# A hybrid gMLP, retention and pooling backbone: where ScalarE writes the normalised tiles of the pooling layer

## The reference

```python
def _rms_norm(x, gain):
    xf = x.astype(jnp.float32)
    y = xf * lax.rsqrt(jnp.mean(xf * xf, axis=-1, keepdims=True) + EPS)
    return (y * gain.astype(jnp.float32)).astype(x.dtype)

def _pool_mixer(h, w_pool, pool_scale):          # h: normed and modulated tokens
    ...
    for g, w in enumerate(POOL_WINDOWS):         # windows 2, 4, 8, 16
        lo = jnp.clip(t - w // 2, 0, length)
        hi = jnp.clip(t + w // 2, 0, length)
        mean = (csum[:, hi, g] - csum[:, lo, g]) / (hi - lo)
        outs.append(mean - hg[:, :, g])
    pooled = jnp.stack(outs, axis=2).astype(h.dtype)
    y = jnp.einsum('blgc,gcd->blgd', pooled, w_pool).reshape(bsz, length, D_MODEL)
    return y * pool_scale
```

## Time and profile before

| | us |
|---|---|
| median of 3 runs | 2644.5 |
| lowest, highest | 2641.74, 2645.16 |
| the profiled execution | 2645.16 |
| its span in the trace | 2643.4 |
| TensorE busy | 2561.9 (97%) |
| VectorE busy | 1351.4 (51%) |
| ScalarE busy | 593.9 (22%) |
| GpSimd busy | 544.8 (21%) |

### The profile page before, as it was taken

The page is one execution under the profiler, slowest core; times in us unless marked ns, Lnnn a source line. Parts: engine busy times, 40 slices in busy tenths (PEclk is TensorE's granted clock), DMA queues, the critical chain, the costliest instruction groups (busy, mean ns, idle before and its releaser), DMA issues.

```text
span 2643.4 us, 37530 instructions
## 1 busy us (share of the span) xinstructions
PE 2561.9 (97%) x14604; PEld 2240.7 (85%) x14604; DVE 1351.4 (51%) x2366; ACT 593.9 (22%) x982; POOL 544.8 (21%) x230
## 2 busy tenths in 40 slices
PE   7899999979999999999999999999999999999998
PEld 3878899977888888888888888888888888888887
DVE  6635752264385556554556555564444444444445
ACT  3311122142231111111111112751112111121112
POOL 6124321162121212111112111011121211212110
PEclk9999999989999999999999999899999999999999
DMA  7314523274212211211211211011010100101102
GB/s 236 149 67 142 166 96 112 95 265 168 72 33 80 71 56 56 95 56 56 71 56 56 95 56 32 25 32 33 32 48 32 48 32 32 48 32 48 32 32 80
DMA packets 126263, 199.48 MB, mean 75 GB/s; under 512 B 4420, under 2 KB 102504, under 8 KB 125800
## 3 DMA queue, kind: packets, MB, share of 16 engines
q1 hardware_dynamic: 123216, 188.76, 21.1%
q10 hardware_dynamic: 2968, 9.63, 1.2%
HBM read 167.44 MB, written 26.74 MB: 73 GB/s over the span
## 4 chain that ended last, share of the span: by engine, by line
PE 88%; DVE 5%; issue 2%; DMA 2%; ACT 2%; POOL 1%; ACTq 0%; SPq 0%; DVEq 0%; POOLq 0%
PE bank L314 83%; PE bank L1404 1%; PE bank L1432 1%; PE bank L1557 1%; DMA ada_st_in<-in_ada_w_dram 1%; PE bank L1469 1%; DVE ada_acc_in L1053 0%; PE bank L1735 0%; DVE vtok L1107 0%; DMA SB<-state_spill 0%; DVE xgm L1220 0%; POOL ringL L854 0%; DVE h1L L1227 0%; DVE X L1061 0%; ACT pF L736 0%
## 5 line engine op out<-in xcount | busy, mean ns | idle before, releaser
L854 POOL TENSOR_TENSOR ringL<-stage,ringH 128x2048 fp32r<-128x2048 f32 x82 | 392.8, 4790 | 1823.1 <-ACT ringH L532 1823.1
L1061 DVE SCALAR_TENSOR_TENSOR X<-bank,mod,X 128x512 f32<-128x512 f32 (+1 forms) x792 | 515.1, 660 | 363.4 <-PE bank L314 359.1
L314 PE MATMUL bank<-midH,ringH 128*128 128x512 f32 (+1 forms) x1536 | 546.7, 356 | 3.3 <-DVE X L1061 3.3
L314 PE MATMUL bank<-midL,ringH 128*128 128x512 f32 (+1 forms) x1536 | 544.9, 355 | 0.0
L314 PE MATMUL bank<-midH,ringL 128*128 128x512 f32 (+1 forms) x1536 | 544.7, 355 | 0.0
L314 PE MATMUL bank<-hH,ringH 128*128 128x512 f32 (+1 forms) x1248 | 447.2, 358 | 0.2 <-DVE hL L1227 0.2
L314 PE MATMUL bank<-hH,ringL 128*128 128x512 f32 (+1 forms) x1248 | 442.5, 355 | 0.0
L314 PE MATMUL bank<-hL,ringH 128*128 128x512 f32 (+1 forms) x1248 | 442.4, 355 | 0.0
L1336 DVE TENSOR_TENSOR relu<-relu 128x512 f32<-128x512 f32 (+1 forms) x192 | 146.3, 763 | 568.9 <-ACT relu L774 568.8
L774 ACT ACTIVATE relu<-bank 128x512 f32<-128x512 f32 (+1 forms) x192 | 100.9, 527 | 1375.9 <-PE bank L314 1375.9
L314 PEld LDWEIGHTS bank<-midH,ringH 128*128 128x128 f32 x1536 | 291.5, 190 | 46.1 <-DVE X L1061 6.5
(11 more groups left out here) (191 smaller groups left out, 2888.1 us busy)
## 6 DMA issues: line engine op xcount, KB each, us to landing
stage<-in_mlp_w_dram SPq DMA_DIRECT2D x64, 1024.0 KB, 5.3
ada_st_mlp<-in_ada_w_dram SPq DMA_DIRECT2D x18, 1536.0 KB, 8.3
stage<-in_ev_w_in_dram SPq DMA_DIRECT2D x14, 1024.0 KB, 5.1
ada_st_in<-in_ada_w_dram SPq DMA_DIRECT2D x8, 1536.0 KB, 9.5
ada<-in_ada_w_dram SPq DMA_DIRECT2D x8, 1024.0 KB, 13.3
x_spill<-X SPq DMA_DIRECT2D x1, 5120.0 KB, 18.5
gate_spill<-gate_st ACTq DMA_DIRECT2D x8, 640.0 KB, 3.7
gt<-gate_spill SPq DMA_DIRECT2D x20, 256.0 KB, 3.3
```

Of the source, the lines that this page charges most:

```text
L314: mm = nc.tensor.matmul(out, a, b, start=first and n == 0, stop=last and n == 2)
L854: nc.gpsimd.tensor_tensor(ringL[slot][:, :], stage[:, :], ringH[slot][:, :].bitcast(F32), ALU.subtract).then_inc(w_lo, 1)
L1061: V.scalar_tensor_tensor(out=X[:, d, cols(t)], in0=src[:, 0:TB[t][1]], scalar=gate_ap, in1=X[:, d, cols(t)], op0=ALU.mult, op1=ALU.add).th ...
```

## The change

On ScalarE, `pool_tile_hi` of the tiles 2 to 4 and 6 to 8 is issued later: behind the square and the root of the next tile (`FIRST_TILE[1]` is 2, `NT` is 10). Tiles 0 and 1 keep their place; tile 5 follows tile 4 and tile 9 follows tile 8 directly. On VectorE, the reciprocal of tile 2 comes after update 20 and not 19, and its tL after update 21 and not 20. The reciprocal of tile 3 and its tL stay where they were; TensorE's, GpSimd's and SyncE's lists are the same.

```diff
--- before.py
+++ after.py
@@ -85,8 +85,8 @@
 H1_KB = {0: 0, 1: 16, 2: 32}
 HALO = 2 * PADW + P
 LAST_MM_AT = {9: 0, 14: 1, 18: 2, 19: 3, 22: 4, 23: 5}
-LAST_RS_AT = {11: 0, 16: 1, 19: 2, 21: 3}
-LAST_LO_AT = {12: 0, 17: 1, 20: 2, 22: 3}
+LAST_RS_AT = {11: 0, 16: 1, 20: 2, 21: 3}
+LAST_LO_AT = {12: 0, 17: 1, 21: 2, 22: 3}
 POOL_TILE_AT = {("c", 0): 6, ("e", 0): 7, ("e", 1): 8, ("e", 2): 9}
 NORM_AT = {("e", 4): ("tile", 0), ("c", 6): ("tile", 1), ("e", 5): ("row", 0), ("e", 8): ("tile", 2), ("c", 10): ("tile", 3),
            ("e", 9): ("tile", 4), ("c", 11): ("tile", 5), ("e", 10): ("row", 1)}
@@ -804,15 +804,21 @@
         for j in range(6):
             tile_square(2, j)
             pool_sd(j)
-            pool_tile_hi(j)
+            if j < FIRST_TILE[1]:
+                pool_tile_hi(j)
+            elif j > FIRST_TILE[1]:
+                pool_tile_hi(j - 1)
+        pool_tile_hi(5)
         act.wait_ge(gain_ok, 6)
         for n in range(len(UNITS)):
             pooled_hi(n)
             if n < 4:
                 tile_square(2, 6 + n)
                 pool_sd(6 + n)
-                pool_tile_hi(6 + n)
+                if n > 0:
+                    pool_tile_hi(5 + n)
             if n == 3:
+                pool_tile_hi(NT - 1)
                 split_static(U_MLP[1])
             if n == 5:
                 tile_square(3, 0)
```

## The result

| | us |
|---|---|
| median of 5 runs, before | 2643.99 (2641.74 to 2645.16) |
| median of 5 runs, after | 2655.93 (2654.34 to 2659.68) |
| ratio after to before | 1.0052, 95% interval 1.0041 to 1.0063 |
| profiled execution, after | 2655.41, span 2653.6 |
| recorded mean TensorE clock, profiled before and after | 0.988, 0.986 |

What follows compares the result with a forecast made beforehand. Between the two MLPs a chain of short hand-overs was taken to bound the kernel. Rounds of 5.16 us put the weight copy +7.0 or +9.1 later; +8.0 on 2644.5 gave 2652.5 us, range 2648.2 to 2656.8.

Steps and rivals of the forecast that it cites:

- The round: Tiles in two PSUM pairs: the pairs go in turn, one round taking 5.16 us per tile, before 3.3.
- Tiles 2 to 5: First four moved-stage tiles: tile 5 starts at 1659.26 (+3.35), first pF copy at 1665.52 (+5.3 us).
- The copy: Next MLP's weight copy on ScalarE: starts at 1686.4 or 1688.5 against 1679.40, +7.0 or +9.1 us by the clock.
- Removed waits: tH waits for reciprocals on ScalarE: at most 4.4 of 6.8 us go, already inside the sum.
- the 2.67 us from hi of 8 to hi of 9: End of tiles 6 to 9: tile 9's tH comes 2.67 us after tile 8's, its reciprocal queued behind tile 8's tL.
- From there all moves as one piece: Behind the weight copy: order unchanged, a rigid shift to the end, nothing hidden and no further cost.
- The clock term: TensorE ahead of tiles 5 and 6: low clock behind longer stands, so +8.0 taken between +7.0 and +9.1.
- Rival 1: Low clock through all rounds: +1.0 for tiles 8 and 9, +1.5 for one more stretch; +11.6, 2656.1 us; chance 0.12.
- A granted clock low beyond 1675: Changed profile after 1675 us: a low TensorE clock there was listed as a sign the forecast is wrong.

Runs made afterwards that it cites:

- e6: Changed kernel with tL made from tH alone and a PSUM pair freed by tH, not tL (result wrong, time only): 2650.49 us, ratio 1.0016.
- e7: Changed kernel with a third pair of PSUM banks for tile 4, taken from the last four MLP blocks: 2654.48 us, ratio 1.0032.
- e2: Kernel before with VectorE's new places and ScalarE's new order for tiles 2 to 5 only: 2652.14 us, ratio 1.0025.
- e3: Kernel before with ScalarE's new order for tiles 6 to 9 only: 2651.82 us, ratio 1.0024.
- e4: The changed kernel timed again without any edit, against the kernel before: 2655.01 us, ratio 1.0038.
- e5: Changed kernel plus 32 unread matmuls on TensorE, 11 ahead of tile 5, 11 ahead of tile 6, 10 ahead of band 5: 2651.28 us, ratio 1.0025.
- e15: Changed kernel plus only the 10 unread matmuls ahead of band 5: 2653.30 us, ratio 1.0025.
- e1: Kernel before with only VectorE's part of the change, tile 2's reciprocal and tL one update later: 2645.05 us, ratio 1.0002.
- e10: Kernel before plus unread matmuls on TensorE, 2 ahead of tile 6 and 8 ahead of band 5: 2643.10 us, ratio 0.9988.
- e12: Kernel before with later weight copy, pF and pH copies around tH of tiles 6 to 9, reciprocals of tiles 3 and 4 one block sooner: 2639.21 us, ratio 0.9975.
- e11: Kernel before with MLP 1's first weight copy and its VectorE rest moved from after unit 3 to after unit 5: 2640.75 us, ratio 0.9980.

## Why the prediction was wrong: point by point

By the ratio the change cost 5.7 us more than the forecast. The step that failed is the one behind the weight copy (point 5): it was costed at nothing, and the runs show a longer stretch at the low clock there.

1. **The round, right.** I put 5.16 us per tile; 5.04 and 5.01 were measured. The sum has a root of 0.30 in full, and ScalarE starts tH 0.20 behind the root's start (1655.82 to 1656.02): that is most of the 0.15 between them. e6 and e7 show that the ring of two pairs is the cause: tL out of it, 3.70; a third pair, 3.18.
2. **Tiles 2 to 5, right.** First pF +5.3 put, +4.84 measured; tile 5 near 1659.3 put, 1658.58 + 0.49 = 1659.07 measured.
3. **The copy, right.** +7.0 or +9.1 put, +7.45 and +8.77 in two profiled executions, e2 and e3 adding to +7.51. Where in between it falls is decided, as I put it, by the clock at band, product and transposes: all low in e4, while in the first profile the clock was back at 1.00 for tile 7 (1.04 us).
4. **Removed waits, right in direction:** "inside the sum"; 6.8 became 6.1. That tiles 5 and 9 would wait anew (the 2.67 us from hi of 8 to hi of 9) stood in the sum; 2.52 was measured.
5. **"From there all moves as one piece": this step failed.** The text costs everything behind the weight copy at nothing. Measured: +2.3 in the profiled execution (9.76 less 7.45), +7.6 in e4's (16.4 less 8.77). The copy stands 1.90 us on ScalarE ahead of the pF that band 5 waits for; while it does, TensorE stands, now 3.75 us, and then runs at 1.2 GHz for some 8 us more. With this gap filled (e5, e15) the shift is rigid: +0.3 behind the copy in both. In e4 only 2.9 of the 7.6 had come by unit 6; the rest came at two further low stretches, from 1709 and from 1733.
6. **The clock term, mis-sized, and in the wrong place.** Rival 1 had the clock upwards, but as 1.0 us for tiles 8 and 9 and 1.5 for one more stretch. Tiles 8 and 9 ran at full clock (1.06 us each; the window at 1675 has 1.00). The loss was one stretch of some 10 us at 0.50, three times what I took for one, behind a gap whose size before (2.37) I neither showed nor used; and the stretch at tiles 5 to 7 was longer too. "A granted clock low beyond 1675" was one of my own signs of being wrong; it came true at 1687 to 1697, but the kernel before has low stretches beyond 1675 as well, so as a sign it could not tell much.

How large the clock's part is in the median can be seen from the mean clock that is recorded with each execution. Means in us, number of executions in brackets, for 26 executions of before (the session of e1 to e4) and 22 of the changed kernel (its first session):

| recorded clock | 0.984 | 0.985 | 0.986 | 0.987 | 0.988 | 0.989 | 0.990 |
|---|---|---|---|---|---|---|---|
| before | | | 2650.0 (2) | 2648.2 (3) | 2646.0 (9) | 2644.5 (7) | 2642.5 (5) |
| changed | 2659.2 (5) | 2659.9 (5) | 2655.8 (6) | 2655.6 (2) | 2653.9 (4) | | |

At the same clock of 0.988 the change costs 7.9 us, close to the forecast; at 0.987 it is 7.4, at 0.986 5.8 (two executions of before), and e4's three executions at 0.988 (2654.5) give 8.4. The rest goes with a mean clock lower by about 0.0026 (0.9858 against 0.9884), at 1.5 to 1.8 us for each 0.001: some 4 to 5 us, which my forecast left out. This compares executions and is no experiment. The experiments are e5 and e10: the matmuls in the gaps lift the mean clock to 0.9896 and 0.9902, where the kernel before has 0.9883 without them. That the same kernel gave +13.7 and +10.1 is explained only in part. By means, 1.1 us lie between the changed kernel's two sets, and 2.0 us between those of the kernel before (2643.5 and 2645.5), of whose first set the clock of only one execution is recorded.

The Trainium skill (TensorE: Matmul & The Clock Gate, "A second HAM failure mode: psum-queue depth-cycling") says that frequent small idles between groups of matmuls make the clock swing. The low stretch from 1660 to 1670 (0.50 in the window at 1665), behind stands of 0.77 and 2.56 us and with one of 1.98 inside it, agrees in kind. The single stand of 3.75 us ahead of band 5 is another case than the rule's. The rival beside which I had cited it had 0.12.

What stays open: which executions get a further low stretch, and where. Between 1640 and 1740 the first profile of the changed kernel had three (about 10, 10 and 3 us at 0.50; before 7, 3 and 3), e4's had four (14, 10, 7 and 3) with the same instructions; e7's had three (10, 10 and 7); e10 lost one and got another. Nor is it known what sets the length of a stretch: e2's was longer than that of before behind the same gap. One profile for each kernel can't tell whether this is chance or follows from the timing.

## What to carry to other kernels

Two buffers with a reader behind a reader: before an engine's step is put behind the next tile's steps, write down who frees the next tile's buffer. If that is the delayed step itself, two overlapping chains become one, and the wait saved (0.7 us here) is paid back as a longer round (5.0 for 3.3) for every tile. To save such a wait, move the late producer sooner or put independent work into it (e12 has both, their own gain not shown), and take a long copy out from in front of the instruction that TensorE waits for (e11, 5.3 us). And where a shift moves or widens gaps on TensorE, look at the clock behind them as well: in e2 the gap had only moved, and the work behind it still took longer.

## What the runs showed of the hardware that was not expected

- Around a stand of 3.75 us ahead of band 5 the clock was at 0.50 for 10.2 us in each of four profiles (changed kernel, e3, e4, e7). Behind one of 2.37 us it was low for 3.4 us (before, e1) or 6.8 (e2), and behind one of 4.21 us for 6.8 (e6). The work behind a gap can pay for it a second time, but the gap's length alone doesn't say how much.
- Matmuls on idle data in the gap, 0.33 us of it left, kept the clock at 1.00 (e5), at no cost that can be seen at the copy (+7.47 against +7.45). In the kernel before (e10) a low stretch of 6.8 us came later instead, with no stand of over 0.92 us between the filled gap and it.
- A lower mean clock by 0.001 went with 1.5 to 1.8 us of 2650, in both kernels; executions of one kernel differed by 0.004 in it, or some 6 to 7 us, about as much as the round itself cost.
- From VectorE's end to TensorE's start 0.15 us pass, the same in every round; the other hand-overs take about 0.04.
